# Seven half products for part of four convolution layers' gate and value tiles, and six waits moved, in a two-model fp32 forward pass

## The chip, the cores and the metric

One core of one Trainium2 chip runs the whole program. The metric is the device time of one execution in microseconds (us), as the median of several executions. Everything is computed in fp32. The engines are TensorE (PE), VectorE (DVE), ScalarE (ACT), GpSimd (POOL), which here only issues transfers, and SyncE (SP), which issues the stream of weights.

## The reference, cut to what matters

256 tokens of width 1024 go through a first model of two layers (attention mixers, a cross attention to a memory, a gated feed-forward) and then a second model of four layers (a mixer and a convolution feed-forward each). The convolution feed-forward, with `FF_DIM` = 2816, is what most of the change touches:

```python
def conv_ffn(h, w_up, conv_w, conv_b, w_down):
    S = h.shape[1]
    a = h @ w_up                       # 1024 -> 2 * 2816
    pad = jnp.pad(a, ((0, 0), (CONV_W - 1, 0), (0, 0)))
    y = conv_b
    for j in range(CONV_W):            # 3 taps along the tokens
        y = y + conv_w[j] * pad[:, j:j + S, :]
    gate, val = jnp.split(y, 2, axis=-1)
    return (jax.nn.silu(gate) * val) @ w_down
```

In the second model `mod = silu(c) @ ada_w[i] + ada_b[i]`, a vector of 6144 numbers per layer, shifts, scales and gates each half of a layer.

## The kernel before, in words

Activations lie feature-major: `x` and `h` are 8 blocks of 128 features by 256 tokens. Each weight matrix is cut into 128x128 tiles, which SyncE streams in the order of use into a ring of 11 slabs of 8 tiles; a slab is loaded again once TensorE has released it (`slab_used`). `make_plan` lists all projections (`Linear`), numbers their output groups and gives each group its PSUM bank. A projection of kind "F" computes one 128-feature output tile after another, each as K products of 128x128 by 256 tokens, into two banks in turn (`linear`, `whole`). `head` and `tail` tiles are done in two halves of 128 tokens, so that the norm before them (in halves too) and the norm after them overlap with matmuls. Every fp32 product is two MATMUL records in the trace.

Kind "S" (`seven`) does two output tiles at a time as a 2x2 block product: features in even and odd blocks, tokens in two halves, seven products of half size in place of eight (28 of 128 columns for K = 8, where 16 of 256 columns would do the same). It needs sums of the moving operand, once per projection (`moving_sums`, four VectorE operations), four sums of weight tiles for each pair (`up_weights` or `down_weights`, read from the ring by VectorE), and afterwards ScalarE's `first_copy` and VectorE's `combined` (four operations) to form the two tiles from four PSUM slots. Pairs use the bank pairs 5, 6 and 7, 3 in turn. Before the change the feed-forwards of the first model (up0, up1), all second projections (down0, down1, cdown0 to cdown3) are of kind "S"; the convolution layers' first projections (cup0 to cup3, 44 tiles of K = 8) are of kind "F" with two head tiles.

In a cup stage ScalarE makes the first tap and the bias of a tile from PSUM (L1180), VectorE adds the other two taps (L1680, L1682), ScalarE makes the silu of a gate tile, and VectorE multiplies by the value tile (L1687). All 22 gate tiles come first, then all 22 value tiles. Between the tiles VectorE forms the modulation of a later layer: `ada_tile` (L1710) multiplies a 128x1024 tile by silu(c) and sums; 192 such tiles come through a ring of three buffers, loaded by POOL's queue, 38 of them in each of cup0 to cup2 and none in cup3.

POOL's queue also loads what the layers need now and then. `gm_rows(1)` loads 3 MB for the last mixer into a region that is free after the mixer of layer 2; POOL then waited for its landing before it issued the next ada tile (L479 to L481).

Other waits that the change touches: `bank_free` waits until both halves of a tail tile have been added by VectorE, though the second halves are in other banks (`LATE`). `h_ready` places the second token half's sum of squares (`norm_sum(norm, 1)`) in TensorE's order behind ten half-width products of the head. In `memory`, `residual("memo...")` begins with `before`, the first `up_weights`. `up_tiles` forms a sum of down weights ahead of the last gated tile. `mem_source(1)`, eight VectorE operations for the memory of layer 1, stands ahead of `up_tiles(0)`. In a down pair TensorE releases the first pair's weight tiles with the first product of the second pair.

## Time and profile before

| | us |
|---|---|
| median of 3 runs | 2610.83 |
| lowest, highest | 2610.54, 2617.75 |
| the profiled execution, its time | 2622.73 |
| the profiled execution, its span from first to last instruction | 2620.9 |

The profiled execution is the one from which all rows below come. Its mean granted TensorE clock is 0.966 of full speed. A slice of the busy line or a share is an average over stages with different limits, so that a wait is to be read where it stands.

### The profile page before, as it was taken

To read this page: it belongs to the slowest core of one execution; us is meant where nothing else is said; L and a number is where in the kernel's file an instruction comes from. 1 tells how busy PE (TensorE), PEld (TensorE's weight loads), DVE (VectorE), ACT (ScalarE), POOL (GpSimd) and SP (SyncE) were. 2 spreads that over 40 slices of the span, in tenths; PEclk is the share of its full clock that TensorE was granted. 3 is DMA by queue.
4 is the path that set the end of the run, shared out by engine and by line. 5 is a ranking of instruction groups with operands and counts; after the bars stand their busy time and mean duration, and the time that the engine had idled before them with its cause. 6 is when DMAs were issued, how large, how long until landed. Compare 5 with 4: busy or idle time off the path is not lost.

```text
span 2620.9 us, 38049 instructions
## 1 busy us (share of the span) xinstructions
PE 2484.9 (95%) x14704; PEld 2054.0 (78%) x14704; DVE 1472.4 (56%) x3034; ACT 512.1 (20%) x1297; POOL 111.1 (4%) x212
## 2 busy tenths in 40 slices
PE   7898999998898999999999899999999999999997
PEld 4465999755558998689889588898787897689897
DVE  4744787456546885333676445763845674333363
ACT  2221110024311101112211332102222101102210
POOL 0000000000000000000110001100001100000000
PEclk9879999996799999999999999999999999999999
DMA  6123456630125556535776147764227774434432
GB/s 229 67 97 141 154 209 234 217 131 1 37 104 193 209 188 247 177 121 193 281 264 243 71 163 279 279 235 162 103 97 278 283 263 155 174 123 145 152 121 97
DMA packets 122351, 453.30 MB, mean 173 GB/s; under 512 B 13776, under 2 KB 13904, under 8 KB 121680
## 3 DMA queue, kind: packets, MB, share of 16 engines
q1 hardware_dynamic: 92880, 338.24, 35.7%
q0 software_dynamic: 29312, 112.80, 12.2%
q8 instruction: 117, 1.92, 0.3%
q14 instruction: 42, 0.34, 0.0%
HBM read 449.93 MB, written 1.05 MB: 172 GB/s over the span
## 4 chain that ended last, share of the span: by engine, by line
PE 82%; DVE 10%; DMA 3%; ACT 3%; issue 2%; SPq 0%; POOL 0%; DVEq 0%; ACTq 0%
PE pair L517 65%; PE bank L517 16%; DMA ring<-stream_dram 2%; DVE att_s L1596 1%; DVE h L1377 1%; DVE arena L1591 1%; DVE adat L1710 1%; ACT arena L1128 1%; DVE rstd L1374 1%; DVE arena L1473 1%; ACT arena L1140 1%; DMA arena<-gmws_dram 1%; PE bank L739 0%; DMA adat<-adaw_dram 0%; DVE arena L2048 0%
## 5 line engine op out<-in xcount | busy, mean ns | idle before, releaser
L517 PE MATMUL pair<-h,ring 128*128 128x256 f32 (+1 forms) x4352 | 875.8, 363 | 24.6 <-DVE x L1404 6.8
L517 PEld LDWEIGHTS pair<-h,ring 128*128 128x128 f32 x4352 | 772.8, 191 | 123.1 <-DVE arena L1682 9.2
L517 PE MATMUL pair<-arena,ring 128*128 128x128 f32 (+1 forms) x2432 | 386.1, 319 | 12.6 <-DVE x L1404 7.5
L517 PEld LDWEIGHTS pair<-arena,ring 128*128 128x128 f32 x2432 | 352.5, 194 | 43.8 <-DVE x L1404 8.3
L517 PE MATMUL pair<-ring,h 128*128 128x512 f32 (+1 forms) x768 | 325.9, 582 | 3.0 <-DVE h L1377 3.0
L517 PE MATMUL pair<-arena 128*128 128x128 f32 (+6 forms) x2178 | 271.3, 299 | 11.8 <-ACT arena L1119 3.6
L517 PEld LDWEIGHTS pair<-ring,h 128*128 128x128 f32 x768 | 142.5, 191 | 170.6 <-issue 163.8
L517 PEld LDWEIGHTS pair<-arena 128*128 128x128 f32 (+3 forms) x2178 | 229.6, 193 | 47.9 <-issue 25.6
L1710 DVE CUSTOM_DVE_ANT_0 adat<-adat,crow,cols 128x1024 f32<-128x1024 f32 x192 | 244.0, 1277 | 22.1 <-DMA adat<-adaw_dram 21.9
L517 PE MATMUL bank<-arena 128*128 128x128 f32 (+2 forms) x1976 | 239.5, 297 | 14.7 <-ACT arena L1140 7.9
L517 PEld LDWEIGHTS bank<-arena 128*128 128x128 f32 (+2 forms) x1976 | 211.7, 191 | 39.7 <-ACT arena L1140 18.4
L1680 DVE SCALAR_TENSOR_TENSOR arena<-pair,cols,arena 128x255 f32<-128x255 f32 x176 | 84.8, 482 | 228.8 <-ACT arena L1180 228.8
L517 PE MATMUL bank<-arena,ring 128*128 128x128 f32 x1636 | 193.5, 275 | 2.5 <-DVE arena L1518 2.3
L517 PEld LDWEIGHTS bank<-arena,ring 128*128 128x128 f32 x1636 | 187.9, 192 | 3.6 <-DVE arena L1518 3.1
L1180 ACT ACTIVATE arena<-pair,cols 128x256 f32<-128x256 f32 x176 | 99.3, 564 | 466.4 <-PE pair L517 466.4
L1537 DVE COPY arena<-pair 128x512 f32<-128x512 f32 (+1 forms) x58 | 39.3, 677 | 224.3 <-PE pair L517 224.2
L474 POOL DMA_DIRECT2D adat<-adaw_dram x192 | 101.5, 529 | 1277.9 <-DVE mod L1710 1238.2
L1098 ACT ACTIVATE h<-x 128x256 f32<-128x256 f32 x84 | 32.9, 413 | 341.2 <-DVE x L1405 144.6
L1405 DVE SCALAR_TENSOR_TENSOR x<-pair,fin,x 128x256 f32<-128x256 f32 (+1 forms) x40 | 17.2, 431 | 141.9 <-PE pair L517 141.9
L1473 DVE TENSOR_TENSOR arena<-ring 128x512 f32<-128x512 f32 (+4 forms) x64 | 58.2, 914 | 54.2 <-DMA ring<-stream_dram 52.2
L1682 DVE SCALAR_TENSOR_TENSOR arena<-pair,cols,arena 128x254 f32<-128x254 f32 x176 | 84.7, 482 | 6.3
L1128 ACT ACTIVATE arena<-arena,att_s 128x256 f32<-128x256 f32 (+2 forms) x160 | 67.6, 423 | 97.7 <-DVE att_s L1596 96.6
(225 smaller groups left out, 1837.4 us busy)
## 6 DMA issues: line engine op xcount, KB each, us to landing
ring<-stream_dram SPq DMA_DIRECT2D x638, 512.0 KB, 4.4
adat<-adaw_dram POOLq DMA_DIRECT2D x192, 512.0 KB, 4.4
arena<-gmrows_dram POOLq DMA_DIRECT2D x2, 2560.0 KB, 11.2
arena<-cmpw_dram POOLq DMA_DIRECT2D x1, 2112.0 KB, 8.2
x<-x_in_dram SPq DMA_DIRECT2D x2, 512.0 KB, 4.7
arena<-mem_in_dram SPq DMA_DIRECT2D x1, 1024.0 KB, 12.9
arena<-gmws_dram POOLq DMA_DIRECT2D x2, 512.0 KB, 13.2
out_dram<-h POOLq DMA_DIRECT2D x2, 512.0 KB, 3.8
```

The costliest lines, as they stand in the source:

```text
L474: pool.dma_start(adat[:, n % ADA_RING, :], adaw_d[n]).then_inc(sem(f"ada_in{n % ADA_RING}"), 16)
L517: return nc.tensor.matmul(out, lhsT, rhs, start=start, stop=stop)
L1098: nc.scalar.activation(h[:, k, :], x[:, k, :], ACT.Square).then_inc(sem("sq_done"), 1)
L1128: ins = nc.scalar.activation(p, p, ACT.Exp, bias=att_s[:, u % 3, 0, e:e + 1], accum_out=att_s[:, u % 3, 1, e:e + 1])
L1140: ins = nc.scalar.copy(pT[:, u % 2, :, :].rearrange("p a q -> p (a q)"), tb[:, :])
L1180: nc.scalar.activation(ybuf[:, t % 4, :], banks[g % 2][:, 0:TOK], ACT.Identity, bias=col(f"conv_b{i}", t), scale=col(f"conv_w{i}", 2 * 2 * ...
L1374: V.reciprocal(rstd[:, 1, cols], rstd[:, 0, cols]).then_inc(sem("rstd_read"), 1)
L1473: ins = V.tensor_tensor(s[0], part(2, a, b), part(3, a, b), ALU.add)
L1537: V.tensor_copy(dst(n % 2, n // 2 * 512, w), banks[g % 2][:, 0:w]).then_inc(sem("freed_dve"), 1)
L1680: link(V.scalar_tensor_tensor(y[:, 1:TOK], b[:, 0:TOK - 1], col(f"conv_w{i}", 2 * FT + t), y[:, 1:TOK], ALU.mult, ALU.add))
L1682: V.scalar_tensor_tensor(y[:, 2:TOK], b[:, 0:TOK - 2], col(f"conv_w{i}", t), y[:, 2:TOK], ALU.mult, ALU.add).then_inc(sem("freed_dve"), 1)
L1710: V.tensor_tensor_reduce(out=w, in0=w, in1=crow[:, :], scale=1.0, scalar=col(f"ada_b{i}", t), op0=ALU.mult, op1=ALU.add, accum_out=mod[:, ...
```

## The change

cup0 to cup3 become kind "S". Their tiles run in order of t: the head is now gate tile 0 and value tile 0 (it was gate tiles 0 and 1), then for each t the gate and the value tile t, either as a pair of seven half products or as two whole tiles. In cup0 to cup2 t = 2, 4, ..., 18 are pairs (9), in cup3 t = 2, 3, 5, 6, ..., 20 (13). The moved waits: POOL does not wait for `gm_rows` and issues `gm_rows(1)` six ada tiles later; `bank_free` takes `x_half` for tail tiles; the second `norm_sum` comes three half-width products earlier; the first `up_weights` of a feed-forward moves from the start of memo's residual to between its two halves; `mem_source(1)` moves into `up_tiles(0)`; the last gated tile of an up stage comes ahead of the down sums; and the first pair of a down projection waits for its last sum one product earlier and releases its tiles there.

```diff
+        plan += [Linear(f"cup{i}", "S", DK, 2 * FT, "dve"), Linear(f"cdown{i}", "S", FT, DK, "dve")]
...
+            if grows:
+                rows = [(t, FT + t) for t in range(1, FT)]
+                paired = SEVEN.get(lin.name, range(FT))
+                lin.units = [("half", (0, FT))]
+                for row in rows:
+                    lin.units += [("pair", row)] if row[0] in paired else [("one", row[:1]), ("one", row[1:])]
+            else:
+                lin.units = [("pair", (n, n + 1)) for n in range(0, lin.N - TAIL, 2)]
+                lin.units.append(("tail", tuple(range(lin.N - TAIL, lin.N))))
             lin.ktiles = [(j, min(KBLOCK, lin.K // 2 - j)) for j in range(0, lin.K // 2, KBLOCK)]
+            lin.pairs, lin.at = [], {}
             lin.pair0 = counts[grows]
...
+SEVEN = {f"cup{i}": range(2, 19, 2) for i in range(LAYERS2 - 1)}
+SEVEN[f"cup{LAYERS2 - 1}"] = [t for t in range(2, 21) if t % 3 != 1]
...
+        HALF_FREED = {}
+        for name, source in SOURCE.items():
+            lin = PLAN[source]
+            for n in range(TAIL):
+                HALF_FREED[FREER[lin.g0 + lin.groups - TAIL + n][1]] = TAILS[name] + n + 1
...
                 pool.wait_ge(sem("gm_free"), 1 + j)
                 pool.dma_start(view(QT, GMROW), gmrows_d[j]).then_inc(sem("gm_in"), 16)
                 pool.dma_start(gm_ws, gmws_d[j]).then_inc(sem("gm_in"), 16)
-                pool.wait_ge(sem("gm_in"), 32 * (1 + j))
...
             gm_rows(0)
-            ada_tiles(ADA_T // 2 + ADA_RING, 3 * ADA_T + ADA_RING)
+            ada_tiles(ADA_T // 2 + ADA_RING, 3 * ADA_T + 3 * ADA_RING)
             gm_rows(1)
-            ada_tiles(3 * ADA_T + ADA_RING, LAYERS2 * ADA_T)
+            ada_tiles(3 * ADA_T + 3 * ADA_RING, LAYERS2 * ADA_T)
+            pool.wait_ge(sem("gm_in"), 64)
...
                 for engine, n in BANK_WAITS[g].items():
-                    pe.wait_ge(sem("freed_" + engine), n)
+                    if engine == "dve" and n in HALF_FREED:
+                        pe.wait_ge(sem("x_half"), HALF_FREED[n])
+                    else:
+                        pe.wait_ge(sem("freed_" + engine), n)
...
+                def whole(t, g):
+                    bank_free(g)
+                    for k in range(lin.K):
+                        last = mm(banks[USED[g][0]][:, 0:TOK], tile(t + k), moving(k), k == 0, k == lin.K - 1)
+                        release(last, k < lin.K - 1, t + k)
+                    last.then_inc(sem("mm_done"), 1)
...
-                    if not lin.head:
+                                  t + 2 * lin.K if not grows and p else None)
+                    if not grows:
                         ins.then_inc(sem("down_read"), 1)
                         summed(1)
                     ins = product(two, 1, lambda j: own[2][:, j, :], lambda j: sums[:, 2, j, :])
-                    if not lin.head:
-                        ins.then_inc(sem("down_read"), 1)
-                        summed(2)
-                    ins = product(one, 2, lambda j: own[1][:, j, :], lambda j: sums[:, 1, j, :])
-                    if not lin.head:
+                    if not grows:
                         ins.then_inc(sem("down_read"), 1)
                         summed(3)
+                    ins = product(one, 2, lambda j: own[1][:, j, :], lambda j: sums[:, 1, j, :], None,
+                                  t + 2 * lin.K if not grows and p == 0 else None)
+                    if not grows:
+                        ins.then_inc(sem("down_read"), 1)
                     ins = product(two, 2, lambda j: own[3][:, j, :], lambda j: moving(2 * j + 1)[:, HALVES[1]])
...
                     else:
-                        late = i == 0 and n == 1 and k == 2
+                        late = i == 0 and n == 0 and k == DK - 1
                     if late and norm not in ("mem0", "mem1"):
                         norm_sum(norm, 1)
...
-                    linear(f"cup{i}", hin, h_ready(f"ffn2_{i}"), head=HEAD)
+                    up_ready = h_ready(f"ffn2_{i}")
+                    seven(f"cup{i}", hin, upT[1], lambda at, k, half: at is not None and up_ready(at, k, half),
+                          MOVING_SUMS[f"cup{i}"] + 1)
...
+                paired = {ns[0]: g for ns, _, g in lin.pairs}
+                tapped = sum(len(PLAN[f"cup{j}"].pairs) for j in range(i))
+
+                def first_tap(t, w):
+                    n = t + FT * w
+                    if t >= 2:
+                        act.wait_ge(sem("hid_done" if w else "conv_gate"), FT * i + t - 1)
+                    if t in paired:
+                        act.wait_ge(sem("freed_dve"), FREER[paired[t]][1])
+                        e = list(paired).index(t) % 2
+                        source = high[:, e, 2 * w:2 * w + 2, :].rearrange("p a q -> p (a q)")
+                    else:
+                        act.wait_ge(sem("mm_done"), lin.at[n] + 1)
+                        source = banks[USED[lin.at[n]][0]][:, 0:TOK]
+                    nc.scalar.activation(ybuf[:, (2 * t + w) % 4, :], source, ACT.Identity,
+                                         bias=col(f"conv_b{i}", n), scale=col(f"conv_w{i}", 2 * 2 * FT + n)
                                          ).then_inc(sem("conv_first"), 1)
 
                 def gate(t):
-                    act.wait_ge(sem("freed_dve"), FREER[lin.g0 + t][1])
-                    nc.scalar.activation(hid[:, t, :], ybuf[:, t % 4, :], ACT.Silu).then_inc(sem("conv_gate"), 1)
-
-                for t in range(2 * FT + 1):
-                    if t < 2 * FT:
-                        first_tap(t)
-                    if 0 <= t - 1 < FT:
+                    if t in paired:
+                        act.wait_ge(sem("pair_tapped"), 2 * (tapped + list(paired).index(t)) + 1)
+                    else:
+                        act.wait_ge(sem("freed_dve"), FREER[lin.at[t]][1])
+                    nc.scalar.activation(hid[:, t, :], ybuf[:, 2 * t % 4, :], ACT.Silu).then_inc(sem("conv_gate"), 1)
+
+                for t in range(FT + 1):
+                    if t in paired:
+                        first_copy(paired[t], high[:, list(paired).index(t) % 2])
+                    if t >= 1:
                         gate(t - 1)
+                    if t < FT:
+                        first_tap(t, 0)
+                        first_tap(t, 1)
 
...
                     add_squares(DK - TAIL, HALVES[i], DK - TAIL + TAIL * i + 1)
+                    if i == 1 and between_halves is not None:
+                        between_halves()
                     normalise(norm, gain, i)
...
                 q = up_pairs[0]
                 up_pairs[0] += 1
-                base = lin.tile0 + lin.K * len(lin.head) + 2 * lin.K * (q - lin.pair0)
+                base = UP_PAIRS[q][0]
                 if q >= 2:
-                    dve.wait_ge(sem("mm_done"), PLAN[f"up{(q - 2) // (FT - 1)}"].g0 + 3 + (q - 2) % (FT - 1))
+                    dve.wait_ge(sem("mm_done"), UP_PAIRS[q - 2][1] + 1)
...
                 for t in range(1, FT):
+                    if t == 3 and early is not None:
+                        early()
                     if t + 2 < FT:
-                        up_weights(i)
+                        up_weights()
                     combined(lin.g0 + 1 + t, ebuf[:, t % 2]).then_inc(sem("freed_dve"), 1)
                     if t >= 2:
                         gated(t - 1)
                     if t % 2 == 0:
                         ada_tile()
-                down_weights(f"down{i}")
                 gated(FT - 1)
-                for _ in range(3):
+                for _ in range(4):
                     down_weights(f"down{i}")
...
+                paired = {ns[0]: g for ns, _, g in lin.pairs}
+                tapped = sum(len(PLAN[f"cup{j}"].pairs) for j in range(i))
+                dve.wait_ge(sem("h_done"), H_DONE[f"ffn2_{i}"] + TT * DK)
+                moving_sums(h, upT[1], 0, DK // 2)
+
+                def taps(t, w, source, signal):
+                    n = t + FT * w
+                    y = ybuf[:, (2 * t + w) % 4, :]
+                    dve.wait_ge(sem("conv_first"), 2 * (FT * i + t) + w + 1)
+                    link(V.scalar_tensor_tensor(y[:, 1:TOK], source[:, 0:TOK - 1], col(f"conv_w{i}", 2 * FT + n),
                                                 y[:, 1:TOK], ALU.mult, ALU.add))
-                    V.scalar_tensor_tensor(y[:, 2:TOK], b[:, 0:TOK - 2], col(f"conv_w{i}", t),
-                                           y[:, 2:TOK], ALU.mult, ALU.add).then_inc(sem("freed_dve"), 1)
-                    if t >= FT:
-                        dve.wait_ge(sem("freed_dve"), FREER[g][1])
-                        dve.wait_ge(sem("conv_gate"), FT * i + t - FT + 1)
-                        V.tensor_tensor(hid[:, t - FT, :], hid[:, t - FT, :], y, ALU.mult).then_inc(sem("hid_done"), 1)
-                        for j, w in PLAN[f"cdown{i}"].ktiles:
-                            if t - FT == 2 * (j + w) - 1:
-                                dve.wait_ge(sem("hid_done"), FT * i + t - FT + 1)
-                                moving_sums(hid, downT, j, w)
-                    if t >= 2 * FT - 2:
+                    V.scalar_tensor_tensor(y[:, 2:TOK], source[:, 0:TOK - 2], col(f"conv_w{i}", n),
+                                           y[:, 2:TOK], ALU.mult, ALU.add).then_inc(sem(signal), 1)
+
+                def gated(t):
+                    if t in paired:
+                        dve.wait_ge(sem("pair_tapped"), 2 * (tapped + list(paired).index(t)) + 2)
+                    else:
+                        dve.wait_ge(sem("freed_dve"), FREER[lin.at[FT + t]][1])
+                    dve.wait_ge(sem("conv_gate"), FT * i + t + 1)
+                    V.tensor_tensor(hid[:, t, :], hid[:, t, :], ybuf[:, (2 * t + 1) % 4, :], ALU.mult
+                                    ).then_inc(sem("hid_done"), 1)
+                    for j, w in PLAN[f"cdown{i}"].ktiles:
+                        if t == 2 * (j + w) - 1:
+                            dve.wait_ge(sem("hid_done"), FT * i + t + 1)
+                            moving_sums(hid, downT, j, w)
+
+                for t in range(FT):
+                    if t + 2 in paired:
+                        up_weights()
+                    if t in paired:
+                        e = high[:, list(paired).index(t) % 2]
+                        combined(paired[t], e).then_inc(sem("freed_dve"), 1)
+                        if i + 1 < LAYERS2:
+                            ada_tile()
+                    for w in range(2):
+                        if t in paired:
+                            taps(t, w, e[:, 2 * w:2 * w + 2, :].rearrange("p a q -> p (a q)"), "pair_tapped")
+                        else:
+                            taps(t, w, banks[USED[lin.at[t + FT * w]][0]], "freed_dve")
+                            if i + 1 < LAYERS2:
+                                ada_tile()
+                    if t >= 1:
+                        gated(t - 1)
+                    if t >= FT - 3 and i + 1 < LAYERS2:
+                        ada_tile()
+                    if t >= FT - 2:
                         down_weights(f"cdown{i}")
-                    if t % 7 != 6 and i + 1 < LAYERS2:
-                        ada_tile()
+                gated(FT - 1)
                 for _ in range(2):
                     down_weights(f"cdown{i}")
...
-                residual(f"memo{i}", f"ffn{i}", col(f"norm_ffn{i}", 0, DK), before=lambda: up_weights(i))
+                residual(f"memo{i}", f"ffn{i}", col(f"norm_ffn{i}", 0, DK), between_halves=up_weights)
...
-                mem_source(1)
-                up_tiles(0)
+                up_tiles(0, lambda: mem_source(1))
```

## Rows read from the trace of the kernel before

**Rows 1.** The page, part 1: busy time of each engine, share of the span.
```profile
PE 2484.9 (95%) x14704; PEld 2054.0 (78%) x14704; DVE 1472.4 (56%) x3034; ACT 512.1 (20%) x1297; POOL 111.1 (4%) x212
```

**Rows 2.** Waits of TensorE, whole span: total us, times, longest.
```profile
PE pair L517 <- DVE x L1404: 17.9, 6, 3.8
...
PE pair L517 <- DVE arena L1682: 5.5, 1, 5.5
...
PE pair L517 <- ACT h L1111: 4.6, 5, 0.9
...
PE pair L517 <- DVE x L1405: 3.8, 2, 1.9
...
PE bank L517 <- DVE arena L1479: 3.5, 3, 1.8
...
PE pair L517 <- DVE arena L1479: 3.1, 2, 1.6
...
PE bank L517 <- DVE arena L1518: 2.3, 2, 1.2
...
PE pair L517 <- DVE arena L1518: 1.4, 3, 0.7
```

**Rows 3.** Timeline of cup0, steady: start, length, engine, [idle before <- releaser].
```profile
1302.04 0.56 ACT L1180 ACTIVATE arena<-pair,cols 128x256 f32<-128x256 f32 x1 [2.89 <-PE pair L517]
...
1302.64 0.48 DVE L1680 SCALAR_TENSOR_TENSOR arena<-pair,cols,arena 128x255 f32<-128x255 f32 x1 [0.79 <-ACT arena L1180]
...
1303.67 0.42 DVE L1687 TENSOR_TENSOR arena<-arena 128x256 f32<-128x256 f32 x1
...
1304.02 1.28 DVE L1710 CUSTOM_DVE_ANT_0 adat<-adat,crow,cols 128x1024 f32<-128x1024 f32 x1
...
1305.49 0.56 ACT L1180 ACTIVATE arena<-pair,cols 128x256 f32<-128x256 f32 x1 [2.89 <-PE pair L517]
```

**Rows 4.** Timeline of up1, two pair starts and VectorE's work for one.
```profile
857.45 1.95 PE L517 MATMUL bank<-h,ring 128*128 128x128 f32 x16
...
857.65 0.69 DVE L1477 TENSOR_TENSOR arena<-ring 128x512 f32<-128x512 f32 x1 [0.52 <-PE pair L517]
...
860.32 0.41 DVE L1524 TENSOR_TENSOR arena<-pair,arena 128x256 f32<-128x256 f32 x1
...
861.76 0.42 DVE L1649 TENSOR_TENSOR arena<-arena 128x256 f32<-128x256 f32 x1
...
863.70 1.95 PE L517 MATMUL pair<-h,ring 128*128 128x128 f32 x16
```

**Rows 5.** Timeline of up1's start, VectorE: the moving sums, then the next operation.
```profile
824.05 0.69 DVE L1515 TENSOR_TENSOR arena<-h 128x512 f32<-128x512 f32 x1
...
826.72 0.68 DVE L1477 TENSOR_TENSOR arena<-ring 128x512 f32<-128x512 f32 x1
```

**Rows 6.** Timeline of cup0's start, second half of h and of the head.
```profile
1217.63 2.45 ACT L1111 ACTIVATE h<-h,mod 128x128 f32<-128x128 f32 x8 [1.41 <-DVE h L1377]
...
1218.08 5.14 PE L517 MATMUL pair<-h,ring 128*128 128x128 f32 x35 [0.93 <-ACT h L1111]
...
1221.25 0.48 DVE L1680 SCALAR_TENSOR_TENSOR arena<-pair,cols,arena 128x255 f32<-128x255 f32 x1 [1.82 <-ACT arena L1180]
```

**Rows 7.** Chain of waits in cup0: start, length, what; a tap begun without a wait.
```profile
1353.38 0.41 DVE arena L1680
```

**Rows 8.** Timeline of memo1's start.
```profile
796.73 0.69 DVE L1477 TENSOR_TENSOR arena<-ring 128x512 f32<-128x512 f32 x1 [4.37 <-DMA ring<-stream_dram]
...
799.87 11.77 PE L517 MATMUL pair<-arena,ring 128*128 128x256 f32 x48 [3.71 <-DVE x L1404]
```

**Rows 9.** Timeline of up0's head.
```profile
274.56 4.63 PE L517 MATMUL pair<-h,ring 128*128 128x128 f32 x20 [3.41 <-DVE x L1404]
```

**Rows 10.** Timeline of cup2 behind the transfers of gm_rows(1).
```profile
1989.71 1.28 DVE L1710 CUSTOM_DVE_ANT_0 adat<-adat,crow,cols 128x1024 f32<-128x1024 f32 x1 [8.52 <-DMA adat<-adaw_dram]
...
1991.97 6.33 PE L517 MATMUL pair<-h,ring 128*128 128x256 f32 x17 [5.50 <-DVE arena L1682]
```

More of the change, by code:

```diff
@@ L141, in tiles_of @@
     if lin.kind == "S":
-        out = [(k, n) for n in lin.head for k in range(lin.K)]
-        for a, b in lin.pairs:
-            out += [(2 * j + e, n) for n in (a, b) for e in range(2) for j in range(lin.K // 2)]
-        return out + [(k, n) for n in lin.tail for k in range(lin.K)]
+        out = []
+        for kind, ns in lin.units:
+            if kind == "pair":
+                out += [(2 * j + e, n) for n in ns for e in range(2) for j in range(lin.K // 2)]
+            else:
+                out += [(k, n) for n in ns for k in range(lin.K)]
+        return out
     if lin.kind == "T":
@@ L613, in half, with pair @@
                     return last
[L615 to L625 removed]
+                grows = lin.K < lin.N
+                half_k = lin.K // 2
+                def whole(t, g):
[4 more added lines that the diff above has]
+                    last.then_inc(sem("mm_done"), 1)
+                def pair(p, t, g):
                     q = lin.pair0 + p
[L627 removed]
+                    own = [upW[:, q % 2, m] for m in range(4)] if grows else downW[name != "down0"]
                     bank_free(g)
```

114 lines of the change are left out of this document (49 added, 65 removed).

## The prediction

> **What bounds the kernel now.** I read the page first: TensorE is busy for 2484.9 of 2620.9 us, 95% [rows 1]. So only two things can pay: fewer columns streamed through TensorE, and fewer of its waits. The second view is TensorE's list of waits [rows 2]. The reader is to see that the six groups that the moved waits concern are short and repeated. The third view is the timeline of a cup stage [rows 3]: the first tap starts at 1302.04 and again at 1305.49, so a whole tile takes 3.45 us, while VectorE and ScalarE stand idle for TensorE each time. TensorE never pauses in between. The fourth is the timeline of an up stage, which already works with half products [rows 4]: pairs start at 857.45 and 863.70, 6.25 us apart, for 56 records, 0.1117 us each.
>
> **The change part by part: what it takes away.**
>
> Products. Two whole tiles take 2 x 3.45 = 6.90 us and a pair 6.25, so a pair gives 0.65. There are 3 x 9 + 13 = 40: 26.0 us.
>
> The start of memo. VectorE stood before the first up_weights for 4.37 us, for a slab of the ring, and TensorE therefore for 3.71 [rows 8]; memo0 does the same (3.8 is the longest of its group in [rows 2]). The 48 records behind it, 32 of 256 and 16 of 128 columns, would take 32 x 0.216 + 16 x 0.112 = 8.7 us, and take 11.6 before the next begins: 2.9 us more, at the lower clock (1.2 GHz). With up_weights between the halves, its slab has long landed. Gain 2 x (3.75 + 2.9) = 13.3.
>
> up0's head. Its 20 records of 128 columns would take 2.2 us and take 4.4, since the 3.41 us pause before them was followed by the lower clock [rows 9]. The pause is broken up now, so I take 2.0; not less than 0, not more than 2.2.
>
> The second halves. The remaining waits on x L1404 are two of 3.4 and two of 1.8 us (17.9 less 7.5 and 6.8), those on x L1405 two of 1.9 [rows 2]. TensorE now starts on the first bank at once, but soon stands in norm_sum until VectorE and ScalarE have squared the second halves. What is gained is what norm_sum moves forward. For the two heads of up it is nothing: up_weights, 860.32 - 857.65 = 2.67 us [rows 4], now stands in front of the second normalise. For the two memk I take 1.2 each of 1.8, for the two on L1405 1.5 each of 1.9. Of the five waits of 0.9 on h L1111 the other three gain three products, 3 x 0.22, 2.0 in all. Sum 7.4, between 0 and 17.9 - 7.5 + 3.8 + 2.8 = 17.
>
> Up to down: the two waits of 1.2 on L1518 go, as the gated tile no longer stands behind a down sum: 2.3. The wait of 0.7 for mem_source(1) goes [rows 2]; its operations then lie in up0, where VectorE has to spare. Five waits on L1479, 6.6 us together, come from the third down pair's sums, which waited for slabs that the first pair held to its end. They are released two products of 11 tiles earlier, 4.9 us, more than the longest wait of 1.8: 6.6.
>
> gm_rows(1). VectorE stood 8.52 us for an ada tile issued only after 3 MB had landed, TensorE 5.50, and the next 17 records took 6.33 in place of 3.67 us [rows 10]: 8.2 in all. Now the 3 MB are issued with three ada tiles in hand and the next is wanted some 14 us later. It is late by about 2 us, which the two banks and the pair behind it cover. If that cover fails, up to 5 come back.
>
> Together 26.0 + 13.3 + 2.0 + 7.4 + 2.3 + 0.7 + 6.6 + 8.2 = 66.5 us.
>
> **What it adds.** The head of each cup stage. The last h is ready at 1217.63 + 2.45 = 1220.08 [rows 6]. Today the first taps (1221.25, two operations) free the bank at 1222.3, just as TensorE is through with the head. Now VectorE makes moving_sums first, 826.72 - 824.05 = 2.67 us [rows 5], then up_weights for t = 2, 2.67, and only then the taps, 1.0: 1226.4. ScalarE's first tap, TensorE's tile t = 1 and all that follows are queued behind it. TensorE waits 4.2 us, four times: 16.8. This is the largest term against the change, and nothing hides it: tile 1 needs bank 0 or 1, both full.
>
> The clock after it. Each pause of 3.7 us and more in the rows was followed by slow records [rows 8, 10]; of the two of 3.4 us one was [rows 9]. I take 2.8 us four times, 11.2, between 0 and 4 x 2.9.
> The Trainium skill ("TensorE: Matmul & The Clock Gate", section "Why this matters for your kernels") warns against idle gaps between bursts of matmuls, after which TensorE is back at the lower clock. By that rule both pauses of 3.4 us would have been followed by it, and the rows show one; for the four heads rule and rows give the same 11.2 against this change.
>
> The middle of a cup stage. For a pair tile and a whole one TensorE needs 6.25 + 6.90 = 13.15 us. VectorE needs: up_weights 2.67 and combined 861.76 - 860.32 = 1.44 [rows 4]; four times two taps of 1.03 with the wait between (1303.67 - 1302.64), 4.1; two products of 0.35 and three ada tiles of 1.25 [rows 3], 4.5; a quarter of the sums for down, 0.7: 13.4. Where a tap follows another operation without waiting, it is 0.41 to the next and not 0.52 [rows 7], which gives 12.9. So VectorE goes from less than two thirds busy to level with TensorE. Two banks and a pair of slack take up a lag of 2 us, so I take 0 here, between 0 and 9 x 0.3 a layer, 8 in all. cup3 has no ada tiles and room.
>
> The end of a cup stage. After the last value tile of cup0 to cup2 VectorE has: a lead of 0.6 for the first tap, taps 1.0, ada 1.2, product 0.35, ada 1.2, a down sum of 11 tiles 1.8 (2.67 / 4 x 11 / 4), the last product 0.35, the last moving sums 2.0 (3/4 of 2.67): 8.5, and it comes to this about 0.5 late. TensorE has 44 records to do, 4.9, and waits 4.1; today it waits 0.5. cup3, without ada tiles: 6.1 - 4.9 = 1.2. Sum 3 x 3.6 + 1.2 = 12. For the clock after it I take 2.5, half of three falls' 2.6 each and a little less, as the pause is split in three.
>
> Together 16.8 + 11.2 + 12.0 + 2.5 = 42.5.
>
> **Sum.** 66.5 - 42.5 = 24 us gained. The profiled execution (2622.7 us, its span 2620.9 with 1.8 around it) would be 2598.7. The median of the runs is 11.9 lower than it; nothing in the change touches what makes that up, so 2610.8 - 24 = 2587.
>
> **The rivals.**
>
> A, no fall of the clock. The pauses in front of the cup tiles stay under what lowers it. For it: one pause of 3.4 us without a fall. Against: all of 3.7 and more had one. It gives back 11.2 + 2.5: 2573.
>
> B, the ends are later. Nine ada tiles in the last three t, at 4.4 us each to land and three buffers, meet the refilled ring; the first down sum of each end waits for slabs, as VectorE did for 4.37 us [rows 8], and all behind it on VectorE with it. Three times 4.4: 2587 + 13 = 2600.
>
> C, the moved waits turn into others. Of the 24.5 us of second halves, up to down, third pair and gm_rows, half is taken by the next wait in line: 2599. For it: norm_sum already eats most of the first. Against: for the third pair the release is 3 us earlier than it needs be.
>
> D, slower: VectorE becomes the bound of cup0 to cup2. A pair's taps can't start before ScalarE's first tap, and that not before combined; each costs 0.60 (1302.64 - 1302.04, [rows 3]). If both are laid bare, a step of two t takes 13.4 + 1.2 = 14.6 and not 13.15, 27 times 1.45, 39 us: 2626. It decides from 14.05 us a step on (24 us over 27 steps). Against it: an ada tile of 1.25 stands between combined and the taps and covers the first, and the second is done meanwhile.
>
> That the products don't get cheaper at all can't well be: the up stages show the same pair at 6.25 us.
>
> **How the numbers follow.** Forecast 0.45 (its own range 2578 to 2595), A 0.22, B 0.20, C 0.07, D 0.04, anything else 0.02. 80% lies between 2570 and 2603: A with a little more gain at the low end, B at the high end; a bare middle of cup (8 us) and a gm_rows cover that fails (5) lie in it. A measurement can tell 0.3% here, 7.8 us: faster means below 2603. Forecast and A are, of B and C most: 0.89 faster, 0.06 the same, 0.05 slower.
>
> **What would show it.** In the profile after: pairs in cup 6.25 us apart and whole tiles 3.45; at the start of each cup an idle of 4.2 us before tile t = 1, released by a tap of VectorE, and records at the lower clock behind it; at the end of cup0 to cup2 waits of 4 us in all, released by L1518's successor; no wait on a ring slab at memo; no wait of TensorE for the third down pair; no 5.5 us wait in cup2. VectorE's share goes from 56% to about 61%, 40 times 2.67 + 1.44. The forecast is wrong if TensorE waits inside the steps of a cup, if the pause at the head is below 3 us, or if the memo stall comes back between the halves.

## The result, and the profile after

The changed kernel takes 2598.2 us (median of 5 runs, 2594.7 to 2600.9) where the kernel before took 2613.5 beside it (5 runs): ratio 0.9936, 95% interval 0.9915 to 0.9956. Timed again beside the experiments it took 2596.0, ratio 0.9919 (0.9905 to 0.9932), about 21 us less. Profile against profile it is 2599.6 against 2622.7, 23.2 less.

Part 1 of the page after answers to [rows 1]: TensorE is busy 19 us less, VectorE 156 us more. Its share is 63%, where the forecast said 61%; its own terms, 40 x (2.67 + 1.44) = 164 us on top of 1472, give 63 too.

```profile
PE 2465.8 (95%) x15664; PEld 2070.3 (80%) x15664; DVE 1628.3 (63%) x3370; ACT 522.0 (20%) x1337; POOL 111.0 (4%) x212
```

TensorE's waits, as [rows 2] (total us, times, longest). L1740 is the second tap, L1749 the gated product, L1570 the last moving sum, L1532 the last weight sum. The groups on the residual's add, 17.9 and 3.8 us before, are gone, and that on ScalarE's h has shrunk from 4.6 to 1.3. A part comes back in front of and in norm_sum: the groups on h L1430, on h L1449 and "issue" (the engine waited for nothing that the profile shows) come to 16.5, where their like came to 7.7 before.

```profile
PE pair L539 <- DVE arena L1740: 16.3, 4, 4.1
...
PE bank L539 <- DVE arena L1749: 7.5, 6, 2.3
...
PE pair L539 <- issue: 6.6, 12, 1.4
PE bank L539 <- DVE arena L1570: 6.4, 4, 1.8
PE pair L539 <- DVE h L1430: 5.2, 3, 3.0
PE bank L539 <- DVE h L1449: 4.7, 7, 0.8
...
PE pair L539 <- ACT h L1152: 1.3, 5, 0.3
...
PE bank L539 <- DVE arena L1532: 0.8, 1, 0.8
```

The head of cup0, all engines, answers to [rows 6]. The last moving sum (1195.90), four weight sums and two taps stand in a row on VectorE, and TensorE resumes as the taps end.

```profile
1191.82 4.32 PE L539 MATMUL pair<-h,ring 128*128 128x128 f32 x32 [0.25 <-ACT h L1152]
...
1195.90 0.69 DVE L1570 TENSOR_TENSOR arena<-h,arena 128x512 f32<-128x512 f32 x1
...
1196.51 0.68 DVE L1530 TENSOR_TENSOR arena<-ring 128x512 f32<-128x512 f32 x1
...
1198.55 0.69 DVE L1532 TENSOR_TENSOR arena<-ring,arena 128x512 f32<-128x512 f32 x1
1199.16 0.48 DVE L1738 SCALAR_TENSOR_TENSOR arena<-pair,cols,arena 128x255 f32<-128x255 f32 x1
...
1200.21 6.10 PE L539 MATMUL pair<-h,ring 128*128 128x256 f32 x16 [4.07 <-DVE arena L1740]
```

The last row has 16 records of 256 columns in 6.10 us, 0.38 each, where 0.216 is usual: the clock is down behind the pause (mean granted clock 0.60 from 1200.3 to 1206.3, 1.00 from 1206.5 on). All four heads wait 4.07.

The middle of cup0, all engines, answers to [rows 3] and [rows 4]. ScalarE's first copy of a pair starts at 1295.02 and at 1308.17: 13.15 us for a pair and two whole tiles, as forecast, and between these TensorE's rows follow each other without a wait.

```profile
1295.02 0.27 ACT L1128 COPY arena<-pair 128x128 f32<-128x128 f32 x1 [5.62 <-PE pair L539]
...
1295.31 0.42 DVE L1576 TENSOR_TENSOR arena<-pair,arena 128x256 f32<-128x256 f32 x1 [0.51 <-ACT arena L1128]
...
1308.17 0.27 ACT L1128 COPY arena<-bank 128x128 f32<-128x128 f32 x1 [5.62 <-PE bank L539]
...
1308.47 0.42 DVE L1576 TENSOR_TENSOR arena<-bank,arena 128x256 f32<-128x256 f32 x1 [0.70 <-ACT arena L1128]
```

Busy us of each engine in the stretch 1205 to 1336 (PE, PEld, DVE, ACT, POOL, then granted clock). VectorE is at 117.89 of 131 us, 90%, TensorE at 100%:

```profile
1205.00:1336.00 131.00, 131.00 (x851) 122.14 (x850) 117.89 (x236) 30.76 (x69) 16.36 (x31) 1.00 0.79 280
```

The end of cup0, TensorE alone: three waits, 3.93 us together, and slow records behind the last (4.35 us for 22 where 2.72 is usual).

```profile
1345.71 2.72 PE L539 MATMUL bank<-arena,ring 128*128 128x128 f32 x22 [1.46 <-DVE arena L1749]
1349.14 0.49 PE L539 MATMUL bank<-arena,ring 128*128 128x128 f32 x2 [0.71 <-DVE arena L1749]
1351.39 4.35 PE L539 MATMUL bank<-arena,ring 128*128 128x128 f32 x22 [1.76 <-DVE arena L1570]
```

The start of memo1, TensorE, answers to [rows 8]: no wait of 3.71 and no slow records. The 0.56 is "issue".

```profile
775.96 12.38 PE L539 MATMUL pair<-arena,ring 128*128 128x256 f32 x64 [0.56 <-issue]
```

The stretch behind gm_rows(1) in cup2, VectorE, answers to [rows 10]. It waits 3.49 us for an ada tile, and TensorE does not wait (8.52 and 5.50 before).

```profile
1998.97 1.28 DVE L1792 CUSTOM_DVE_ANT_0 adat<-adat,crow,cols 128x1024 f32<-128x1024 f32 x1 [3.49 <-DMA adat<-adaw_dram]
```

### The profile page after: what moved, and what is told of

Its sections match the earlier page's. It is cut to its first block, busy times and chain, and to the rows that moved or that the text cites. A ratio compares the mean times of both kernels' runs of the same rounds, so it can differ in the third digit from the quotient of the medians.

```text
span 2597.7 us, 40348 instructions
## 1 busy us (share of the span) xinstructions
PE 2465.8 (95%) x15664; PEld 2070.3 (80%) x15664; DVE 1628.3 (63%) x3370; ACT 522.0 (20%) x1337; POOL 111.0 (4%) x212
## 4 chain that ended last, share of the span: by engine, by line
PE 84%; DVE 8%; ACT 3%; DMA 2%; issue 2%; SPq 0%; DVEq 0%; POOL 0%; ACTq 0%
PE pair L539 61%; PE bank L539 23%; DMA adat<-adaw_dram 1%; DVE att_s L1648 1%; DVE arena L1643 1%; ACT h L1152 1%; ACT arena L1169 1%; DVE rstd L1427 1%; DVE adat L1792 1%; DVE h L1430 1%; ACT arena L1181 0%; PE bank L778 0%; DVE arena L1530 0%; DVE arena L2129 0%; DVE arena L2125 0%
## 5 line engine op out<-in xcount | busy, mean ns | idle before, releaser
L539 PE MATMUL pair<-h,ring 128*128 128x256 f32 (+1 forms) x3424 | 648.4, 349 | 25.2 <-DVE arena L1740 16.3
L539 PEld LDWEIGHTS pair<-h,ring 128*128 128x128 f32 x3424 | 574.9, 193 | 89.0 <-DVE arena L1740 17.0
L539 PE MATMUL bank<-arena 128*128 128x128 f32 (+2 forms) x2584 | 314.1, 295 | 11.3 <-ACT arena L1181 6.9
L539 PE MATMUL pair<-arena 128*128 128x128 f32 (+6 forms) x2530 | 314.3, 296 | 8.7 <-ACT arena L1160 3.6
L539 PEld LDWEIGHTS bank<-arena 128*128 128x128 f32 (+2 forms) x2584 | 283.9, 193 | 36.8 <-ACT arena L1181 17.6
L539 PEld LDWEIGHTS pair<-arena 128*128 128x128 f32 (+4 forms) x2530 | 270.8, 193 | 45.3 <-issue 23.0
L539 PE MATMUL bank<-arena,ring 128*128 128x128 f32 x1912 | 235.4, 280 | 14.0 <-DVE arena L1749 7.5
L1526 DVE TENSOR_TENSOR arena<-ring 128x512 f32<-128x512 f32 (+5 forms) x104 | 85.7, 827 | 43.3 <-DMA ring<-stream_dram 29.2
L1530 DVE TENSOR_TENSOR arena<-ring 128x512 f32<-128x512 f32 (+5 forms) x104 | 85.9, 829 | 34.8 <-PE bank L539 24.1
L1532 DVE TENSOR_TENSOR arena<-ring,arena 128x512 f32<-128x512 f32 (+5 forms) x104 | 86.2, 832 | 5.0 <-PE bank L539 0.8
L1528 DVE TENSOR_TENSOR arena<-arena,ring 128x512 f32<-128x512 f32 (+5 forms) x104 | 86.2, 832 | 4.2 <-PE bank L539 0.8
```

Source lines behind the costliest of these rows:

```text
L539: return nc.tensor.matmul(out, lhsT, rhs, start=start, stop=stop)
L1526: ins = V.tensor_tensor(s[0], part(2, a, b), part(3, a, b), ALU.add)
L1528: ins = V.tensor_tensor(s[1], s[0], part(0, a, b), ALU.subtract)
L1530: ins = V.tensor_tensor(s[2], part(0, a, b), part(2, a, b), ALU.subtract)
L1532: ins = V.tensor_tensor(s[3], part(1, a, b), s[1], ALU.subtract)
```

## Experiments

Twelve kernels ran in three sets, each with its own runs of the kernel before (2618.8, 2617.1 and 2621.1 us). "To before" is the ratio with its 95% interval.

**a0_after_again.** The changed kernel, unedited.

> The changed kernel itself, unchanged, beside the kernel before on one chip. Theory 1: the stages of its trace sum up to 20 us less than before without what lies ahead of the first change, so a ratio of 0.992. Rival (the 24 us of the forecast hold and the first five runs of before were on the low side): 0.9908 or below.

Measured 2596.0, to before 0.9919 (0.9905 to 0.9932): 21 us gained. The others are held against this, ratio against ratio. The interval of such a difference is 5 to 9 us to either side, so the traces are read beside it. In them the time from cup0's head to the end is the steady part: 1392.2 and 1393.0 us in the two traces of the changed kernel, 1389.3 before.

**p1_pairs_only.** All moved waits put back, the new plan of the cup stages kept.

The cut shows three of them: the first up_weights ahead of memo's residual, POOL's wait, the place of norm_sum.

```diff
...
+                if before is not None:
+                    before()
...
+                pool.wait_ge(sem("gm_in"), 32 * (1 + j))
...
-                        late = i == 0 and n == 0 and k == DK - 1
+                        late = i == 0 and n == 1 and k == 2
...
```

> The kernel with the convolution pairs but with all six moved waits put back as before. Theory 1 (the pairs cost more than they give): 26 us given, 42.5 taken, 16.5 us slower than before, about 2630 us. Rival (the pairs are worth their 26 us and the moved waits give little or nothing): about 2590 us, faster than before.

Measured 2623.9, 1.0025 (1.0008 to 1.0043): 6.6 us lost, not 16.5. Its trace has all four head waits, 4.07, and the end waits, but neither the 5.5 us wait of cup2 nor a wait at the third pair in cdown0 to cdown2. The kernel before had both, 8.2 us with the clock and 4.9, and the expected 16.5 counts them as there: without them it would be 3.4.

**p2_no_pairs.** The moved waits kept, no pair and no moving sums in a cup stage, tiles still in order of t. The ada tiles are spread anew, with their number per stage kept.

```diff
-SEVEN = {f"cup{i}": range(2, 19, 2) for i in range(LAYERS2 - 1)}
-SEVEN[f"cup{LAYERS2 - 1}"] = [t for t in range(2, 21) if t % 3 != 1]
+SEVEN = {f"cup{i}": [] for i in range(LAYERS2)}
...
```

> The changed kernel with all convolution tiles whole (no pairs, no moving sums for them), in the new order of tiles and with all six moved waits. Theory 1: the moved waits give 40.5 us, the late end of cup0 to cup2 stays and takes 11 of it; 29 us faster than before, about 2584 us, and faster than the changed kernel. Rival (pairs carry the gain): slower than the changed kernel by the 26 us of products less nothing, 2620 us or above.

Measured 2591.7, 0.9892 (0.9861 to 0.9923), 28 less than before. The gain comes without any pair; the pairs, as they are put in here, cost some 7 us of it. 28.3 less 6.6 is 21.7, and the whole change gives 21.1: the two parts add up. Both runs have the new order of tiles, so this holds only if the order by itself is worth next to nothing, and it wasn't run alone.

**e1_half_head, e2_full_head.** In a cup stage the first `up_weights` (e1), or it and the moving sums (e2), go behind the taps of t = 0.

```diff
                 for t in range(FT):
-                    if t + 2 in paired:
+                    if t and t + 2 in paired:
                         up_weights()
...
+                    if t == 0:
+                        dve.wait_ge(sem("h_done"), H_DONE[f"ffn2_{i}"] + TT * DK)
+                        moving_sums(h, upT[1], 0, DK // 2)
+                        up_weights()
                     if t >= 1:
                         gated(t - 1)
```

(This is e2's, which also removes this wait and the moving sums from the start of the stage; e1 puts only `up_weights()` there.)

> The changed kernel, but only the first weight sums (2.67 us) go behind the taps of tile 0; the moving sums stay ahead of them. Theory 1 with the clock as a step: the four waits shrink from 4.35 to about 1.7 us and no slow records follow, 4 x (2.67 + 2.8) = 22 us, 2576 us. Rival (the slow records follow any wait at this place): only 4 x 2.67 = 10.7 us, 2587 us, with the clock's fall still in the trace behind each head.

> The changed kernel, but at the start of each convolution stage VectorE takes both taps of tile 0 first, and makes the moving sums and the first weight sums after them. Theory 1 (the head pause and the clock behind it are the largest cost of the change): the four waits of 4.35 us before tile 1 go, and with them the slow records behind them, 4 x (4.2 + 2.8) = 28 us; about 2570 us where the changed kernel takes 2598. Rival (VectorE is level with TensorE inside these stages, so work put off at the head comes back as waits of TensorE inside the stage or at its end): less than 10 us, 2590 or above, with new waits of TensorE on taps at t = 3 to 7.

e1: 2578.5, 0.9838 (0.9807 to 0.9869). e2: 2571.7, 0.9807 (0.9774 to 0.9840), 29 us better than the change by the ratios, where the forecast's terms for head and clock are 28. From cup0's head to the end its trace is 22.8 us shorter than that of the change, and e1's 20.1; 29 against 28 is closer than the runs can tell. Of the rival's new waits inside the stages there are two in e2, 0.66 and 1.42 us, both in cup2. TensorE at the same place of cup0, first e1, then e2:

```profile
1193.45 4.32 PE L539 MATMUL pair<-h,ring 128*128 128x128 f32 x32 [0.26 <-ACT h L1152]
1199.19 8.96 PE L539 MATMUL pair<-h,ring 128*128 128x256 f32 x48 [1.42 <-DVE arena L1740]
```

```profile
1194.37 13.18 PE L539 MATMUL pair<-h,ring 128*128 128x128 f32 x80 [0.26 <-ACT h L1152]
```

With 1.42 us of pause 48 records take 8.96 us; in the change, after 4.07, they take 11.34. So half a head fix also removes the whole clock term. The 48 records behind the other three heads take 10.64, 11.39 and 11.43 us in the change, and 8.96 in e1: e1 gains 4 x 2.65 of wait and 9.0 of clock, 19.6; the ratios say 21.

**e3_end, e4_head_end.** The last gated product goes ahead of all but one down sum, and ada tiles leave the last t for the places between the down sums; e4 is e3 with e2.

```diff
-                            if i + 1 < LAYERS2:
+                            if i + 1 < LAYERS2 and t < FT - 1:
                                 ada_tile()
...
-                    if t >= FT - 3 and i + 1 < LAYERS2:
+                    if t == FT - 3 and i + 1 < LAYERS2:
                         ada_tile()
-                    if t >= FT - 2:
+                    if t == FT - 2:
                         down_weights(f"cdown{i}")
                 gated(FT - 1)
-                for _ in range(2):
+                for n in range(3):
                     down_weights(f"cdown{i}")
+                    for _ in range((1, 1, 2)[n] if i + 1 < LAYERS2 else 0):
+                        ada_tile()
```

> The changed kernel, but at the end of each convolution stage the last taps, the last two products and the last moving sums come ahead of four ada tiles and of one down sum, which follow between the remaining down sums. Theory 1 (TensorE's waits of 4 us at the start of cdown0 to cdown2 come from that queue on VectorE): they go, 3 x 3.9 us, with a fall of the clock behind them of 1 to 3 us each, 13 to 18 us less than the changed kernel. Rival B (the ada tiles' transfers and the ring are late there, whatever the order): less than 5 us, and the waits reappear one pair later, at the down sums.

> The changed kernel with both orders of VectorE put right: taps of tile 0 ahead of the moving sums and first weight sums, and the end of the stage as in the run before this one. Theory 1: both gains add, 28 and 15 us, some 43 us less than the changed kernel, ratio to before 0.976. Rival (VectorE is level with TensorE inside the stages, and the head's work is only given back later): the two don't add, at most 30 us less, with waits of TensorE inside the stages.

e3: 2594.2, 0.9915 (0.9899 to 0.9930), 1 us better than the change by the ratios, 4 to 5 by the traces from cup0's head on. e4: 2566.6, 0.9803 (0.9788 to 0.9818), 30 us better than the change and not 43, the best kernel of the study, though hardly ahead of e2. The waits at the end are gone and one of the same size stands at the second pair of cdown, as the rival of e3 had it. TensorE in e4:

```profile
1340.93 9.99 PE L539 MATMUL bank<-arena 128*128 128x128 f32 x88
1350.76 7.53 PE L539 MATMUL pair<-arena,ring 128*128 128x128 f32 x66
1362.31 13.01 PE L539 MATMUL pair<-arena 128*128 128x128 f32 x88 [4.02 <-DVE arena L1532]
```

and VectorE there, held up by an ada tile's transfer ahead of the sum that TensorE waits for. Six ada tiles of 1.2 us each stand in this queue from 1345 on, and no sum of the second pair waits for the ring:

```profile
1353.65 1.28 DVE L1796 CUSTOM_DVE_ANT_0 adat<-adat,crow,cols 128x1024 f32<-128x1024 f32 x1 [3.18 <-DMA adat<-adaw_dram]
...
1360.48 1.69 DVE L1532 TENSOR_TENSOR arena<-ring,arena 128x512 f32<-128x512 f32 x2
```

**e5_ada_later.** e4 with the ada tiles of the end in the second and third pair of cdown.

```diff
-                    for _ in range((1, 1, 2)[n] if i + 1 < LAYERS2 else 0):
-                        ada_tile()
...
-                    down_ada = ada_tiles((2, 1, 1, 1, 1, 1, 1, 1, 1))
+                    down_ada = ada_tiles((0, 0, 0, 2, 2, 1, 3, 3, 3))
```

> The full reordering of the head and the last products ahead of the down sums (as in e4_head_end), and the ada tiles of each convolution stage's end leave it: none stands between the down sums or in the three places of the first down pair; the second pair gets 2, 2, 1 and the third 3, 3, 3. Theory (the ends' waits are VectorE's load: ada tiles of 1.25 us, and the waits for them to land, stand ahead of the second pair's last sum): the first sums end some 9 us earlier, the three waits of 4.3, 4.6 and 5.7 us and the slow records behind them (3 us each) go, 22 us less than e4_head_end: 2545, ratio to before 0.972. Rival (the sums wait for the slabs of the ring, whatever VectorE does besides): waits of 3 us and more stay at the second pair, and the time stays at 2562 to 2567. Second rival: the nine tiles of the third pair land too slowly and the modulation of the next layer is late: a new wait ahead of the norm, 2552 to 2560.

Measured 2582.1, 0.9851 (0.9832 to 0.9870): 13 us worse than e4. The wait at the second pair is gone (so ada tiles had made it), and two others come, in each of cdown0 to cdown2. TensorE, then VectorE:

```profile
1379.74 11.69 PE L539 MATMUL bank<-arena 128*128 128x128 f32 x88 [2.52 <-DVE arena L1532]
...
1405.71 2.93 PE L539 MATMUL bank<-arena,ring 128*128 128x128 f32 x12 [4.46 <-DVE x L1475]
```

```profile
1363.79 1.62 DVE L1526 TENSOR_TENSOR arena<-ring 128x1408 f32<-128x1408 f32 x1 [7.04 <-DMA ring<-stream_dram]
...
1374.03 1.28 DVE L1794 CUSTOM_DVE_ANT_0 adat<-adat,crow,cols 128x1024 f32<-128x1024 f32 x1 [3.46 <-DMA adat<-adaw_dram]
...
1390.94 1.29 DVE L1794 CUSTOM_DVE_ANT_0 adat<-adat,crow,cols 128x1024 f32<-128x1024 f32 x1 [5.03 <-DMA adat<-adaw_dram]
```

Nine tiles in one pair come too slowly through three buffers: the second rival of this run, dearer than it had it. VectorE also waits 7.04 for the ring at 1363.79 without anything queued ahead of that sum, so the third pair's sums are late by the ring as well as by the ada tiles between them; the two weren't parted.

**u1_memo.** The first `up_weights` back ahead of memo's residual.

```diff
-                    if i == 1 and between_halves is not None:
-                        between_halves()
...
+                if before is not None:
+                    before()
```

> The changed kernel with the first weight sums of a feed-forward back at the start of memo's residual. Theory 1: the two waits of 3.8 us with 2.9 us of slow records behind each come back, 13.3 us more than the changed kernel, and a little more where up's head falls too. Rival C (the slab is late wherever the sums stand): no more than 5 us, as the wait was only moved.

Measured 2605.6, 0.9961 (0.9948 to 0.9973): 11 us more than the change. TensorE waits at memo1 again, and 3.79 at memo0. The 48 records behind take 10.41 and 10.57 where 8.7 is usual, so that the falls of the clock cost 1.7 and 1.9 here and not 2.9; waits and falls make 11.1:

```profile
787.88 10.41 PE L539 MATMUL pair<-arena,ring 128*128 128x256 f32 x48 [3.70 <-DVE x L1457]
```

**u2_gm_wait_back.** POOL's wait and the old place of gm_rows(1).

```diff
+                pool.wait_ge(sem("gm_in"), 32 * (1 + j))
...
-            ada_tiles(ADA_T // 2 + ADA_RING, 3 * ADA_T + 3 * ADA_RING)
+            ada_tiles(ADA_T // 2 + ADA_RING, 3 * ADA_T + ADA_RING)
             gm_rows(1)
```

> The change with one part undone: POOL again waits for the landing of gm_rows, and issues gm_rows(1) six ada tiles earlier. The forecast's term: 8.2 us more than the change, ratio to before 0.995. Rival (the new order of the tiles covers it, as the trace of the pairs alone showed no wait of 5.5 us in cup2): the same as the change within 2 us, 0.992.

Measured 2596.5, 0.9909 (0.9889 to 0.9929): no different from the change. POOL's queue shows the old wait:

```profile
1948.67 0.53 POOL L502 DMA_DIRECT2D arena<-gmws_dram  x1
1960.93 1.05 POOL L496 DMA_DIRECT2D adat<-adaw_dram  x2 [11.73 <-DMA arena<-gmws_dram]
```

but VectorE's fourth ada tile is now wanted at 1966.57, 17.9 us after the issue; before it was wanted at 1981.2, 10.8 us after an issue at 1970.35, and came at 1989.71 [rows 10]. Of the 7.1 us between, 4.2 lie ahead of the first tap (the head's sums) and 2.9 behind it, where TensorE's records are slow after the pause (48 in 11.93 us). So the transfer passes under the head's cost. Whether POOL's wait would cost again with the head put right (e2) wasn't run.

**u3_release_back.** The first down pair waits for its last sum a product later, and its tiles are released with the second pair.

```diff
-                        summed(3)
-                    ins = product(one, 2, lambda j: own[1][:, j, :], lambda j: sums[:, 1, j, :], None,
-                                  t + 2 * lin.K if not grows and p == 0 else None)
+                        summed(2)
+                    ins = product(one, 2, lambda j: own[1][:, j, :], lambda j: sums[:, 1, j, :])
                     if not grows:
                         ins.then_inc(sem("down_read"), 1)
+                        summed(3)
```

> The change with one part undone: the first pair of each down projection again waits for its last sum one product later and releases its tiles with the second pair's first product. The forecast's term: 6.6 us more than the change, 0.9945. Rival (in the convolution layers the later ends hide the third pair's sums, and only down0 and down1 had something to give): 0 to 3 us more, 0.992 to 0.993.

Measured 2606.1, 0.9948 (0.9932 to 0.9965): some 7.6 us more, near the forecast's 6.6, but not where the forecast had it. The group on the last weight sum:

```profile
PE bank L539 <- DVE arena L1532: 4.7, 3, 2.4
```

Its three waits are 1.91 at the third pair of down0, 2.38 at that of down1, and 0.37 in cdown2. Behind each of the first two 88 records take 11.69 us, where 10.06 is usual behind a short wait. Waits and slow records are 7.9 us, where the change has one wait of 0.81. So all of it lies in down0 and down1, the place that the rival of this run named, and nothing to speak of in the convolution layers.

**u4_halves_back.** A tail tile's bank waits for both halves, and the second norm_sum stands three products later.

```diff
-                    if engine == "dve" and n in HALF_FREED:
-                        pe.wait_ge(sem("x_half"), HALF_FREED[n])
-                    else:
-                        pe.wait_ge(sem("freed_" + engine), n)
+                    pe.wait_ge(sem("freed_" + engine), n)
...
-                        late = i == 0 and n == 0 and k == DK - 1
+                        late = i == 0 and n == 1 and k == 2
```

> The change with one part undone: the bank of a tail tile again waits for both halves, and the second norm_sum stands three half-width products later in the heads. The forecast's term: 7.4 us more than the change (0 to 17), ratio to before 0.9947. Rival C's half: 3.7 us more, 0.9933; nothing at all would be 0.992. In the trace waits of 3.4 us released by the residual's add ahead of the heads of up0 and up1, and 1.8 at memk.

Measured 2609.0, 0.9960 (0.9946 to 0.9974): 10.7 us more. TensorE's waits have the old groups again, without memo's two:

```profile
PE pair L539 <- DVE x L1454: 10.4, 4, 3.4
...
PE pair L539 <- ACT h L1149: 4.6, 5, 0.9
PE pair L539 <- DVE x L1455: 3.8, 2, 1.9
```

## Why the prediction was right, and where it was not

The time of TensorE's first record on the second half of h at each cup head divides the run. Before: 1218.08, 1552.63, 1968.16, 2385.38, and 2607.34 for a last mark (norm_sum of the final norm); after: 1191.82, 1531.14, 1949.47, 2362.41, 2584.06; a second trace of the changed kernel (a0): 1182.11, 1522.65, 1940.72, 2354.21, 2575.08.

| stretch | forecast, by its terms | after less before | a0 less before |
|---|---|---|---|
| up to cup0's head | -23.0 | -26.3 | -36.0 |
| cup0's head to cup1's | +2.5 | +4.8 | +6.0 |
| cup1's to cup2's | +1.6 | +2.8 | +2.5 |
| cup2's to cup3's | -4.8 | -4.3 | -3.7 |
| cup3's head to the end | -0.3 | -0.3 | -1.1 |

The forecast's column is its terms laid out by place (for the second: 9 pairs -5.85, head and clock +7.0, end and its clock +4.4, third pair -1.6, second halves -1.5). The whole gain lies ahead of cup0's head, where no pair was added; from there on the changed kernel is 3.0 and 3.7 us slower than before, where the forecast had 1.0 faster, and the kernel without pairs (p2) is 3.4 faster. Point by point:

- **Products.** Right: the step of 13.15 us, with no wait of TensorE inside, is what was forecast for a pair and two whole tiles (6.25 + 6.90). Rival D's case did not come, though VectorE is at 90%.
- **memo.** Right in its waits: forecast 13.3, put back it costs 11. The difference is the clock behind them, 2.9 forecast, 1.7 and 1.9 in u1.
- **Second halves and up0's head.** Forecast 7.4 and 2.0; put back they cost 10.7 together.
- **Third down pair.** Forecast 6.6, put back 7.6, but the nearness is luck. The forecast counted 4.9 of its 6.6 in cdown0 to cdown2; with the old release these show no wait in p1 and 0.37 us in u3. All 7.6 come from down0 and down1, for which it had 1.65 and no fall of the clock. That the later ends of cup0 to cup2 hide the sums fits both runs, and wasn't tested by itself.
- **gm_rows(1).** The step failed: "VectorE stood 8.52 us for an ada tile issued only after 3 MB had landed, TensorE 5.50, [...] 8.2 in all. Now the 3 MB are issued with three ada tiles in hand". The wait is gone with POOL's wait back too (u2, p1): the head's sums and the slow records behind its pause give the transfer the 7.1 us. So its 8.2 us were not the moved wait's to give. The total is untouched, and so with the 4.9 us of the third pair; the split between moved waits and pairs (+16.5 expected for p1, +6.6 measured) is what they shift.
- **Head of cup and clock.** Right: 4.2 forecast, 4.07 found, four times. For the clock 2.8 was forecast, and the slow records cost 2.4, 1.7, 2.4 and 2.5. That is 25.3 us in all against 28; moving the work away gives back 23 by the trace (e2).
- **End of cup.** Forecast 4.1 us of waits in each of three, found 3.93, 4.35 and 4.44 (5.16, 4.91 and 5.18 in a0's trace). The clock behind them was undersized: 2.5 in all, while 22 records take 1.6, 2.3 and 1.6 us too long after cup0, cup1 and cup2, 5.6 in all. Cause as forecast, VectorE's queue with ada tiles in it (e3 to e5). cup3, without ada tiles: 1.2 forecast, 1.17 found.
- **What is not the change's.** The two traces of the one changed kernel differ by 9.7 us ahead of cup0's head. Of these 6.7 lie in the mixer of the first model's second layer (570.89 to 687.53, and 569.35 to 679.25), and the two run the same code. The start differs too: TensorE's second group of records starts at 19.02 and 19.67, before at 20.73. So the first row of the table can't be held against -23.0 to better than some 10 us, and there is one trace of the kernel before. Without that mixer it is -28.1 and -31.1. That the whole comes near -24 is thus in part luck: more gained ahead of the first head than forecast, 4 to 5 us less behind it. Where the second row's +4.8 and +6.0 exceed +2.5, the clock behind the end explains 0.8; the rest is open.

The time itself, 2598.2, is inside the forecast's 80% range and outside its own range of 2578 to 2595; the figures nearest to it are those of B (2600) and C (2599). The step that put the time at 2587 rather than 2598 is the last of the sum: "The median of the runs is 11.9 lower than it; nothing in the change touches what makes that up". Two of the three runs shown were at the low edge of the kernel's own spread: with two runs more its median was 2613.5, beside the experiments 2618.8, 2617.1 and 2621.1, and the profiled execution's 2622.7 was an ordinary one. Profile against profile the forecast was 2598.7, and 2599.6 was found. The forecast of the ratio, 1 - 24 / 2610.8 = 0.9908, lies inside the repeated interval and just under the first.

Of the rivals, A (no fall of the clock) is out by the rows of the four heads. B is not what brought the time near its 2600: at the end of cup0 the first down sum (1339.47) starts without a wait for the ring, the only ada tile that is late there is so by 0.27 us (by 1.0 and 1.4 at most at the ends of cup1 and cup2), and its price of 4.4 us a stage did not come. The waits at the ends are as forecast; late ada tiles show in e3 to e5, once these are put elsewhere. C is true for gm_rows, in another way than it said; of its other three waits, up to down was never put back by itself. D is out by the step of 13.15.

## What to carry to other kernels

Work added ahead of the first operation that frees a bank is paid in full, and again in the clock behind the pause: here 25 us, of which moving eight VectorE operations behind two taps gave back 23. Before a wait is priced as a gain, ask whether the rest of the change would have removed it anyway (gm_rows, and the third pair in three layers). An engine at 90% in a stretch can still take work moved into its middle (e1, e2); at its end, where the next stage's sums are due, the wait only moved along (e3, e5). Judge a forecast by the profile it was made from, and take two traces of one kernel before reading a difference of 10 us between two kernels.

## What the runs showed of the hardware

How long TensorE pauses does not by itself tell whether its clock falls. After 1.41 to 1.42 us in e1's four heads there was no slow record; after 4.07 us in the changed kernel's four heads 48 records took 10.64 to 11.43 us in place of 8.96. In between the rows go both ways. At the down pairs 88 records took 10.06 us behind pauses of 1.83 (before) and 2.40 (e5), and 11.69 behind 1.91 and 2.38 (u3), 2.14 and 2.52 (e5). Of two pauses of 3.41 before, [rows 9] and its twin in up1, one was followed by a fall. A broken-up pause is not safe from it: at the end of cup0 slow records stand behind 1.46, 0.71 and 1.76.

The Trainium skill ("TensorE: Matmul & The Clock Gate", section "Why this matters for your kernels") warns against idle gaps between bursts of matmuls. The trace agrees in the four heads; that pauses of 1.91 to 2.52 us can be enough is not to be had from that rule, and here the measurement decides.
